# Third and fourth modulation step of the recurrent stage moved between the first two units and the first gate product

## What is computed

```python
mods = split((silu_c @ mod_w[l] + mod_b[l])[:, None, :], 6)      # and cmods from silu_cc for the context
zl = modulate(rmsnorm(xl, norm1_g[l]), mods[0], mods[1])
# recurrent mixer, for latent tokens and context tokens
g, xr = split(z @ w_in, 2)                  # w_in: 1024 x 2560
g, x = gelu(g), dwconv(xr, conv_w, conv_b)  # four taps
for d in range(2):                          # forward and backward
    r = sigmoid(block_diag(x, wa[d]) + ba[d])        # 8 blocks of 160 channels
    i = sigmoid(block_diag(x, wx[d]) + bx[d])
    a = exp(-8 * r * softplus(-lam[d]))
    h[d] = scan(a, sqrt(1 - a * a) * (i * x))
y = (g * (h[0] + h[1])) @ w_out
xl = xl + mods[2] * y_lat
zl = modulate(rmsnorm(xl, norm2_g[l]), mods[3], mods[4])
xl = xl + mods[5] * conv_ffn(zl, ...)
```

## Time and profile before

| | |
|---|---|
| time before, median of 3 runs | 3143.56 us (3143.53 to 3145.07) |
| profiled execution | 3143.97 us, span 3142.2 us |
| mean granted clock of TensorE | 0.984 of full |
| PE busy | 3023.6 us (96%) |
| DVE, ACT, POOL busy | 50%, 34%, 11% |
| recurrent stage | about 64 us to 482 us of the span |

### The profile page before, as it was taken

How to read it: one execution, slowest core, us unless ns; L and a number is a source line. 1 busy time by engine, 2 the same in 40 slices (tenths; PEclk the granted TensorE clock), 3 DMA queues, 4 the chain that set the end, 5 groups by cost and what they waited for, 6 DMA issues and landing times. The chain is left out here.

```text
span 3142.2 us, 39947 instructions
## 1 busy us (share of the span) xinstructions
PE 3023.6 (96%) x16999; PEld 2491.5 (79%) x16999; DVE 1581.7 (50%) x1977; ACT 1073.3 (34%) x1276; POOL 355.1 (11%) x378
## 2 busy tenths in 40 slices
PE   5899999999999999999999999999798999999998
PEld 3787878878888888888878888888686788888886
DVE  5667676264444544444573333333426544545545
ACT  4576774141111212211243444344423212222123
POOL 1122221100000000000042222222020000000002
PEclk7999999999999999999999999999899999999999
DMA  6443434122112112111111111110131111111111
GB/s 242 137 140 101 137 92 163 53 85 70 48 60 67 60 62 67 61 54 61 47 59 40 40 40 40 40 40 26 64 98 47 41 47 54 47 47 47 47 48 54
DMA packets 217276, 217.88 MB, mean 69 GB/s; under 512 B 34703, under 2 KB 191982, under 8 KB 210956
## 3 DMA queue, kind: packets, MB, share of 16 engines
q1 hardware_dynamic: 206331, 160.09, 16.8%
q0 software_dynamic: 10704, 55.23, 5.3%
q10 hardware_dynamic: 64, 0.01, 0.0%
HBM read 190.27 MB, written 25.03 MB: 69 GB/s over the span
## 5 line engine op out<-in xcount | busy, mean ns | idle before, releaser
L720 PE MATMUL ps<-zH,wH 128*128 128x512 f32 x2048 | 551.1, 369 | 1.4 <-DVEq L2199 1.4
L720 PE MATMUL ps<-zH,wL 128*128 128x512 f32 x2048 | 548.9, 368 | 0.0
L720 PE MATMUL ps<-zL,wH 128*128 128x512 f32 x2048 | 548.5, 367 | 0.0
L720 PEld LDWEIGHTS ps<-zH,wH 128*128 128x128 f32 x2048 | 353.8, 188 | 84.7 <-issue 16.4
L720 PEld LDWEIGHTS ps<-zH,wL 128*128 128x128 f32 x2048 | 354.1, 188 | 66.8
L720 PEld LDWEIGHTS ps<-zL,wH 128*128 128x128 f32 x2048 | 354.0, 188 | 66.6
L2221 DVE SCALAR_TENSOR_TENSOR res<-ps,mod,res 128x1024 f32<-128x1024 f32 x240 | 236.7, 1014 | 189.6 <-PE ps L720 178.3
L730 DVE SCALAR_TENSOR_TENSOR V<-ps,vec,V 128x1023 f32<-128x1023 f32 x126 | 128.0, 1016 | 375.5 <-ACT V L2080 372.5
L2053 ACT ACTIVATE wH<-wraw 128x1024 fp32r<-128x1024 f32 x130 | 134.6, 1050 | 391.8 <-PE ps L720 391.8
L720 PE MATMUL ps<-hH,wH 128*128 128x512 f32 (+1 forms) x700 | 193.1, 373 | 0.0
L720 PE MATMUL ps<-hL,wH 128*128 128x512 f32 (+1 forms) x700 | 191.0, 370 | 0.0
(11 more groups left out here) (325 smaller groups left out, 4831.7 us busy)
## 6 DMA issues: line engine op xcount, KB each, us to landing
wraw<-in_ffn_w_up_dram SPq DMA_DIRECT2D x88, 512.0 KB, 3.7
modw<-in_mod_w_dram POOLq DMA_DIRECT2D x40, 1024.0 KB, 5.2
wraw<-in_ffn_w_down_dram SPq DMA_DIRECT2D x44, 512.0 KB, 3.7
wraw<-in_na_w_in_dram SPq DMA_DIRECT2D x24, 512.0 KB, 4.8
modring<-in_mod_w_dram SPq DMA_DIRECT2D x8, 1024.0 KB, 10.8
wraw<-in_rg_w_in_dram SPq DMA_DIRECT2D x16, 512.0 KB, 4.8
bias<-scratch_bias SPq DMA_DIRECT2D x32, 224.0 KB, 4.1
scratch_xT<-res SPq DMA_DIRECT2D x8, 640.0 KB, 7.5
```

Of the source, the lines that this page charges most:

```text
L720: last = nc.tensor.matmul(ps[:, slot * SLOT + c:slot * SLOT + c + n], w(k), r(k)[:, c:c + n], start=(k == 0 and i == 0), stop=(k == K - 1 ...
```

## The change

Steps 2 and 3 (the third and fourth) leave their places behind x(0,1) and g(0,0), where `MOD_UNITS` now holds None, and PE does them at the end of `first_pair`, behind step 1 and ahead of the first gate product. On GpSimd's queue their blocks are asked for behind those of steps 0 and 1, ahead of the first stack; the first pass of the loop then asks for no block, and the passes after it ask for the same ones as before (q starts at 4). Each block still goes into the one buffer `modw` and waits for the step before it. Nothing else changes; the order of the additions in the accumulation is the same.

```diff
-    MOD_UNITS = [("x", 0, REM), ("x", 0, 0), ("x", 0, 1), ("g", 0, 0), ("x", 0, 2), ("g", 0, 1), ("x", 0, 3), ("g", 0, 2),
+    MOD_UNITS = [("x", 0, REM), ("x", 0, 0), None, None, ("x", 0, 2), ("g", 0, 1), ("x", 0, 3), ("g", 0, 2),
@@ gpsimd
-        modulation(0)
-        modulation(1)
+        for q in range(4):
+            modulation(q)
         stack(0, 0)
-        q = 2
+        q = 4
         for h in range(2):
             for b in range(NB):
                 whole(h, b)
@@
                     whole(h, REM)
-                modulation(q)
+                if (h, b) != (0, 0):
+                    modulation(q)
                 bias_rows(NB * h + b)
                 if (h, b) != (1, NB - 1):
-                    modulation(q + 1)
-                    q += 2
+                    if (h, b) != (0, 0):
+                        modulation(q + 1)
+                        q += 2
                     store(h, b)
@@ first_pair
                     ins.then_inc(unit_done, 1)
                     modulation(u)
+            modulation(2)
+            modulation(3)
```

## The result

The changed kernel takes 3156.09 us (median of 7 runs, 3153.46 to 3158.27), the kernel before 3143.64 in the runs beside it: a ratio of 1.0034 (95% interval 1.0025 to 1.0044). It is slower by more than the 0.2% that was called the limit. The forecast was 3148.8 with a range up to 3151.3: the sum had the sign right and the size wrong, 5.3 us where 12.4 were measured.

The account below looks back on a forecast made before the run. TensorE, busy 96% of the span, was taken as the bound, its waits the only places to win or lose. +6.4 late start, -1.05 steps gone and 0 clock gave +5.3 us: forecast 3148.8 us, range 3145.0 to 3151.3.

Parts of the forecast that it names:

- The late start: First gate product of the recurrent stage: starts at about 113.8 instead of 107.44, 6.4 us later, with nothing hiding it.
- The third step's landing: In the hole before the first gate product: the third weight block lands 5.2 us after its issue, range 5.0 to 7.9.
- Point 4: Fourth weight block in the hole: asked for at 105.96, lands after 5.4 us at 111.36; its step ends at 113.24.
- Point 5: Stacking DMAs, behind the fourth block on GpSimd's queue: land at 113.8, between the ends 111.2 and 114.
- small bias DMAs: Evidence from elsewhere in the stage: bias DMAs issued behind a modulation block left its landing at 5.3 us.
- rival C: Fourth block shares bandwidth and lands in 7.9 us: first gate product at 115.74, total +7.3, 3150.8 us; chance 0.24.
- The rule of the Trainium skill: DMA queues: descriptors go in ring order, so the stack cannot complete before the block ahead; start 113.96 rather than 113.24.
- The two steps taken off TensorE's path: Two steps leave PE, 2.30 us at full clock; ScalarE's exponent in block (0,1) comes 1.05 us earlier, taken as gain.
- The 1.25 us that PE has left over goes into the wait at 310.57.: At PE's later wait for xL: the part of the 2.30 us not gained there merely lengthens that wait.
- the later wait: PE's wait for xL at 310.57, the second half's start: grows from 2.80 to about 4.0 us.
- not at all (all gained): Sign against the forecast: if the wait at 310.57 does not grow, all 2.30 us of the removed steps are gained.
- The clock: First gate products at half clock: 1.9 us lost before, the same again, so 0; bounds a 1.9 gain, 1 us loss.

Follow-up runs that it names:

- e2: Changed kernel with the first stack asked for behind the third block and ahead of the fourth on GpSimd's queue; ratio 1.0026 to the kernel before.
- e3: Kernel before with only the third modulation step moved ahead of the first gate product, the fourth staying behind g(0,0); ratio 1.0002.
- e4: Changed kernel with a second buffer for the third step's block, so both moved steps fit in the hole; ratio 1.0001 to the kernel before.
- e6: Kernel before without the sixteen matmuls of the third and fourth modulation steps, blocks still loaded; 3148.41 us against 3144.73, ratio 1.0010.
- e7: Changed kernel with a second buffer, and GpSimd's A for REM held until VectorE's pair of gated inputs is through; ratio 0.9999 to the kernel before.
- e10: Kernel before with only the third step moved, one buffer, and GpSimd's A for REM held in both halves; 3143.93 us against 3145.26, ratio 0.9992.
- e9: Changed kernel with GpSimd's A for REM held, first half only, until VectorE made block 3's gated inputs; 3154.86 us, ratio 1.0027 to the kernel before.
- e1: Changed kernel with GpSimd's A for REM held in both halves until VectorE made both gated inputs of block 3; ratio 1.0014 to the kernel before.
- e8: The changed kernel measured once more, with no further edit; 3155.99 us, ratio 1.0032 to the kernel before.
- e5: Kernel before with GpSimd's A for REM held in both halves until VectorE made both gated inputs of block 3; ratio 0.9997.

## Why the prediction was wrong

**The late start** was forecast at +6.4 and is +7.53. The third step's landing (5.2 forecast, 5.1 measured), both half-clock steps (1.88, measured 1.89) and GpSimd's 0.34 us were right. Two steps of the working were too small. Point 4 took 5.4 us for the fourth block; it took 6.9, because a DMA issued behind a block slows it, which the prediction had argued against from small bias DMAs. The stack is three times 160 KB. e2 shows it: moved ahead of the fourth block, the stack slows the third instead. Point 5 let the stack land at 113.96 at the latest; it landed at 108.12 + 7.4 = 115.5, which is 114.8 when the 0.69 us ahead of the first modulation step are taken off. The fourth landing is the term that counts, for the stack held the gate product only 0.26 us longer than the fourth step did. This was rival C in mechanism, with a landing 1.0 us shorter than the 7.9 that it assumed. With a block ahead the stack's three DMAs took 6.6, 7.1 and 7.4 us instead of 2.4 to 3.1; in e2, e3 and e4 they took 6.4 to 7.0. In the changed kernel the block landed at 113.5 and they at 113.7, 114.7 and 115.5. The rule of the Trainium skill that the prediction had weighed (DMA: Bandwidth & Descriptors, section Queues, rings and completion order) has them complete only after the block. These landings agree with it.

**The two steps taken off TensorE's path**: -1.05 forecast for ScalarE's exponent in block (0,1), -1.12 measured, and -1.06 in e6 where nothing else changed. The working of that point was right, up to this mark. It was not a gain at the end of the stage: where the collision stayed away, the clock took it back at the second half's start (e3, e7, e10), and the sum had no term for that.

**What followed from it was wrong**, and this is the step that failed: "The 1.25 us that PE has left over goes into the wait at 310.57." An engine with slack was taken to be harmless when it gets ahead. Even with the collision taken away the sentence does not hold: the wait at the second half is 2.79 us in e9 and 2.80 in e1, no longer than before, and what PE had left over stands in a wait of 1.05 us ahead of the x product of REM. TensorE's lead released GpSimd's A for REM 1.12 us earlier against VectorE's pair (1.22 us behind its start instead of 2.34 in the trace before), ahead of VectorE's second gated input, and that cost 2.75 us on the path, more than the steps had brought. In the prediction's words the later wait was to grow to 4.0; it shrank to 1.25, which its list of signs would have read as a gain of all 2.30 us ("not at all (all gained)") and which was a loss. e9 (the collision taken away, nothing else) and e6 (nothing but TensorE's lead) show the cause from both sides. The Trainium skill (SBUF — State Buffer, section Who interferes with whom) states a rule for this: a VectorE instruction with two inputs in SBUF contends with a GpSimd instruction that reads SBUF, and issue order decides which of them blocks fully. The rows agree in both orders: 5.66 for VectorE's pair when GpSimd began first, 3.44 for GpSimd when VectorE did.

**The clock** was forecast at 0 in the hole and was -0.27 there, within what single executions differ by (e8, the same kernel, took 3.92 us to the first gate tanh where the changed kernel took 4.16). Behind the last input product it cost +1.5, in e8 as well, which the sum did not have at all.

The sum with the measured terms is 7.53 - 1.12 + 2.75 - 0.27 + 1.5 = 10.4, and 0.7 more lies ahead of the first modulation step, where both kernels do the same. The median moved by 12.4. The rest, some 1.4 us, stays open: it is the size of the spread between runs of one kernel (3153.46 to 3158.27). Open too is why e5 and e7 turn 2.9 and 2.5 us at the first sums of squares into 0.3 and 0.5 in the median. A lower clock in the attention stage was seen in e5's trace, but that it is so on average was not shown.

## What to carry to other kernels

Before work is put into an idle stretch, count the transfers that it needs one after the other: a single buffer makes each step a landing plus a step, and here one fitted the hole and two did not. Taking work off an engine that is ahead moves everything that this engine releases; look at which operations of the other engines it brings together, above all a GpSimd operation that begins just before a VectorE operation on the path, and search the trace for operations that take twice their usual time in one block. A gain or loss of a few us per wait can be undone by the clock behind the wait: here moving a step won 1.1 us and a wait of unchanged length, 2.8 us, took 1.3 to 1.5 back at half clock. So read the stage's marks beside the total.

## What was not expected of the hardware

- A GpSimd tensor operation that begins 0.2 us before a VectorE operation with two inputs in SBUF holds it until it has ended: the pair 5.66 us instead of 2.89. In the other order GpSimd takes 3.39 to 3.44 instead of 2.97.
- Three DMAs of 160 KB behind a block of 1 MB on the same queue slow the block (6.2 to 6.9 us, where at the same place it takes 5.1 to 5.6 without them), and themselves take 6.4 to 7.4 instead of 2.4 to 3.1.
- A wait of 2.8 us of TensorE ahead of the second half cost it the clock in five kernels (e9: granted 0.57 from 316 to 320), at a price of 1.25 to 2.7 us, and not in two others: the kernel before and e5 waited 2.80 and 2.78 us at the same place and went on at full clock.
- The place of such a loss decides its price: half clock behind the first of two waits cost nothing in the kernel before, and behind the second it cost 1.5 us in the changed one.
